# The last down-projection of a two-layer hybrid decoder, computed and stored in halves of 256 tokens

## The reference

```python
for l in range(DEPTH):                     # DEPTH 2, x is (1, 512, 1024), float32
    ...                                    # mixers A to D on head groups
    x = x + mixed @ w_out[l]
    h2 = rmsnorm(x, ln2_g[l])
    g = causal_dwconv(h2 @ ffn_w_gate[l], ffn_conv_w[l])
    x = x + (jax.nn.silu(g) * (h2 @ ffn_w_up[l])) @ ffn_w_down[l]   # 2816 -> 1024
return x
```

## Time and profile before

| what | value |
| --- | --- |
| median of three runs | 1314.4 us |
| span of the profiled execution | 1310.8 us |
| what the median has over that span | 3.6 us |
| TensorE busy, of the span | 98% |
| VectorE, ScalarE, GpSimd busy | 65%, 38%, 49% |
| one addition onto x, 128 x 512 | 685 ns |
| stores of x | 8 of 256 KB, median 4.6 us from issue to landing |

### The profile page before, as it was taken

How to read it: one execution, slowest core, us unless ns; L and a number is a source line. 1 busy time by engine, 2 the same in 40 slices (tenths; PEclk the granted TensorE clock), 3 DMA queues, 4 the chain that set the end, 5 groups by cost and what they waited for, 6 DMA issues and landing times.

```text
span 1310.8 us, 15989 instructions
## 1 busy us (share of the span) xinstructions
PE 1290.9 (98%) x6218; PEld 1054.8 (80%) x6218; DVE 849.4 (65%) x1142; ACT 493.5 (38%) x758; POOL 637.2 (49%) x302
## 2 busy tenths in 40 slices
PE   7999999999999999999999999999999999999999
PEld 4888886787888888888878888867878888888887
DVE  8789885846888117775237799677477761377720
ACT  6332556744223112223344245566432221122220
POOL 2986661144444444444468776512444444444442
PEclk9999999999999999999999999999999999999999
DMA  6232331123333323333232322301333233233332
GB/s 222 81 97 65 97 89 33 28 94 113 97 97 115 101 74 97 97 98 110 84 111 82 87 65 92 87 25 53 99 106 97 97 106 103 81 97 97 109 111 87
DMA packets 40939, 120.49 MB, mean 92 GB/s; under 512 B 6432, under 2 KB 10656, under 8 KB 40864
## 3 DMA queue, kind: packets, MB, share of 16 engines
q1 hardware_dynamic: 40864, 119.46, 29.3%
HBM read 114.20 MB, written 2.10 MB: 89 GB/s over the span
## 4 chain that ended last, share of the span: by engine, by line
PE 90%; DVE 5%; ACT 2%; POOL 2%; DMA 1%; issue 1%; SPq 0%; POOLq 0%; ACTq 0%
PE bank L504 26%; PE bank L517 26%; PE bank L509 25%; PE bank L718 3%; PE bank L506 1%; ACT G L1079 1%; PE bank L766 1%; DMA raw<-in_w_in 1%; POOL wl L362 1%; PE bank L663 1%; PE bank L755 1%; DVE G L1568 1%; PE bank L596 1%; PE bank L611 1%; DVE ssum L1196 1%; PE bank L745 1%
## 5 line engine op out<-in xcount | busy, mean ns | idle before, releaser
L362 POOL TENSOR_TENSOR wl<-raw,wh 128x1024 fp32r<-128x1024 f32 (+3 forms) x208 | 507.1, 2439 | 629.4 <-ACT wh L903 385.1
L903 ACT ACTIVATE wh<-raw 128x1024 fp32r<-128x1024 f32 (+3 forms) x208 | 218.6, 1052 | 267.3 <-PE bank L509 207.9
L504 PE MATMUL bank<-xl,wh 128*128 128x512 f32 x1088 | 282.4, 397 | 0.0
L517 PE MATMUL bank<-xh,wl 128*128 128x512 f32 x1088 | 271.1, 391 | 0.0
L509 PE MATMUL bank<-xh,wh 128*128 128x512 f32 x1056 | 261.0, 389 | 0.0
L504 PEld LDWEIGHTS bank<-xl,wh 128*128 128x128 f32 x1088 | 202.8, 188 | 48.2 <-issue 5.9
L517 PEld LDWEIGHTS bank<-xh,wl 128*128 128x128 f32 x1088 | 203.2, 188 | 41.7
L509 PEld LDWEIGHTS bank<-xh,wh 128*128 128x128 f32 x1056 | 198.3, 188 | 41.5
L1230 DVE TENSOR_TENSOR x<-x,bank 128x512 f32<-128x512 f32 x64 | 43.9, 685 | 228.5 <-PE bank L517 228.4
L504 PE MATMUL bank<-ml,wh 128*128 128x512 f32 x512 | 137.5, 395 | 0.0
L517 PE MATMUL bank<-mh,wl 128*128 128x512 f32 x512 | 127.5, 389 | 0.0
(11 more groups left out here) (304 smaller groups left out, 1357.8 us busy)
## 6 DMA issues: line engine op xcount, KB each, us to landing
raw<-in_w_gu SPq DMA_DIRECT2D x88, 512.0 KB, 3.5
raw<-in_w_in SPq DMA_DIRECT2D x52, 512.0 KB, 3.7
raw<-in_w_dn SPq DMA_DIRECT2D x32, 704.0 KB, 4.1
raw<-in_w_ol SPq DMA_DIRECT2D x16, 384.0 KB, 3.1
raw<-in_w_oe SPq DMA_DIRECT2D x16, 256.0 KB, 2.6
x<-in_x SPq DMA_DIRECT2D x8, 256.0 KB, 6.2
raw<-in_w_first SPq DMA_DIRECT2D x4, 512.0 KB, 3.8
out_x<-x SPq DMA_DIRECT2D x8, 256.0 KB, 4.6
```

Of the source, the lines that this page charges most:

```text
L362: tt(wl[:, p, 0:cols], raw[:, p, 0:cols], wh[:, p, 0:cols].bitcast(F32), ALU.subtract).then_inc(wl_full, 1)
L504: mm(bank[b][:, :], wh[:, p, k * P:(k + 1) * P], lo[:, k, :], start=(k == 0), stop=False)
L517: w = mm(bank[b][:, :], wl[:, p, k * P:(k + 1) * P], hi[:, k, :], start=False, stop=(k == K - 1))
L903: fn(wh[:, p, 0:cols], raw[:, p, 0:cols], ACT.Copy).then_inc(wh_full, 1)
```

## The change

In the last down-projection of the last layer the first unit is left as it is on TensorE; the seven others go through a new function, `halved_unit`. It splits the 512 tokens into two halves of 256 and gives each a bank of its own, b and b + 2. In each of the three groups it does the 11 tiles for the first half and then the 11 for the second, and loads the weights of each tile for each half. After the third group's first half it raises `half_done`, after the second `unit_done`. VectorE adds each half when it is done, and SP stores each half by itself: sixteen stores of 128 KB. The first unit's result is added in two halves as well.

```diff
@@ sync @@
             for i in range(KD):
-                sp.wait_ge(resid, L * 4 * KD - KD + i + 1)
-                sp.dma_start(A["out"][:, i, :], x[:, i, :]).then_inc(out_done, 16)
-            sp.wait_ge(out_done, 16 * KD)
+                for part, signal in ((0, half_resid), (1, resid)):
+                    sp.wait_ge(signal, (L * 4 * KD - KD if part else 0) + i + 1)
+                    cols = slice(part * THALF, part * THALF + THALF)
+                    sp.dma_start(A["out"][:, i, cols], x[:, i, cols]).then_inc(out_done, 16)
+            sp.wait_ge(out_done, 32 * KD)
@@ tensor @@
+            def halved_unit(b, K, hi, lo, out):
+                g = next(number)
+                p = g % 2
+                halves = [(bank[b + 2 * i], slice(i * THALF, i * THALF + THALF)) for i in range(2)]
+                pe.wait_ge(wh_full, g + 1)
+                claim(b, out)
+                claim(b + 2, out, 0)
+                for moving in (lo, hi):
+                    for to, cols in halves:
+                        for k in range(K):
+                            w = mm(to[:, 0:THALF], wh[:, p, k * P:(k + 1) * P], moving[:, k, cols],
+                                   start=(k == 0 and moving is lo), stop=False)
+                w.then_inc(wh_free, 1)
+                pe.wait_ge(wl_full, g + 1)
+                for (to, cols), done in zip(halves, (half_done, unit_done)):
+                    for k in range(K):
+                        w = mm(to[:, 0:THALF], wl[:, p, k * P:(k + 1) * P], hi[:, k, cols], start=False, stop=(k == K - 1))
+                    w.then_inc(done, 1)
...
-                units(8, FHALF, mh, ml, resid, hid_ready)
+                if l + 1 < L:
+                    units(8, FHALF, mh, ml, resid, hid_ready)
+                else:
+                    unit(0, FHALF, mh, ml, resid, hid_ready)
+                    for o in range(1, KD):
+                        halved_unit(o % 2, FHALF, mh, ml, resid)
@@ vector @@
+            def half_residual(o, p):
+                for part, done, signal in ((0, half_done, half_resid), (1, unit_done, resid)):
+                    cols = slice(part * THALF, part * THALF + THALF)
+                    dve.wait_ge(done, nth(done))
+                    tt(x[:, o, cols], x[:, o, cols], bank[p + 2 * part][:, 0:THALF], ADD).then_inc(signal, 1)
...
-                    for o in range(KD):
-                        residual(o, o % 2)
+                    dve.wait_ge(unit_done, nth(unit_done))
+                    for part, signal in ((0, half_resid), (1, resid)):
+                        cols = slice(part * THALF, part * THALF + THALF)
+                        tt(x[:, 0, cols], x[:, 0, cols], bank[0][:, cols], ADD).then_inc(signal, 1)
+                    for o in range(1, KD):
+                        half_residual(o, o % 2)
```

More of the change, by code:

```diff
@@ L16 @@
 D, T, P = 1024, 512, 128
+THALF = T // 2
 KD = D // P
@@ L195, in build @@
         unit_done, unit_out, resid = sem("unit_done"), sem("unit_out"), sem("resid")
+        half_done, half_resid = sem("half_done"), sem("half_resid")
         raw_full = [sem(f"raw_full{p}") for p in range(2)]
```

## The result

The changed kernel takes 1317.17 us (median of 13 runs, 1316.53 to 1317.58) where the kernel before took 1314.4 beside it (13 runs, 1313.72 to 1315.99): a ratio of 1.0019 [1.0011, 1.0027], +2.8 us by the medians, +1.4 to +3.5 by the interval. No change (a ratio of 1) lies outside the interval, so the kernel is slower. Against the prediction's own limit, about 0.2% or 1317.0 us, it stands on the edge: the median is just over it, the ratio just inside. The forecast was 1313.8, faster by 0.6; the rival of a fixed price per pair gave 1316.9.

A forecast was written before the change was run, and what follows sets the result against it. TensorE, busy for 98% of a 1310.8 us span, was taken as the bound. Matmuls 0, tail -0.57 and the rest nothing gave -0.6: span 1310.2, with 3.6 around it 1313.8 us; 8-in-10 range 1312.7 to 1317.6.

The forecast's parts named there:

- a fixed price per pair: Rival: each load-and-matmul pair keeps 13 ns over its columns, so doubled pairs cost +3.1; net +2.5 us, 1316.9; chance 0.32.
- What bounds the kernel: Whole kernel: TensorE, busy 98% of 1310.8 us at full clock, ends last nearly everywhere, up to one final VectorE addition.
- The matmuls: Seven halved outputs, 231 loads more: 256-column pairs at 0.1133 us, 7.48 us an output, so 0; range -0.8 to +3.1.
- the third of the three lines: Sum for one output with 13 ns kept per pair: 66 x 0.1200 = 7.92 us, +0.44, seven times +3.1.
- The lower bound: Spacing of 256-column pairs: at least 0.112 us, what a load of 128 columns occupies in plain float32 rows.
- The tail: After the last matmul: last addition halved -0.27 us, last store halved -0.3; together -0.57 (-0.27 to -0.7).
- The rest at nothing: New waits, sixteen stores, fourteen additions, weight-buffer signals: no cost; at most +0.7 us if TensorE's queue were held at each output.
- The load alone: Rival: the weight load sets the pace in halved outputs, 0.112 us a pair; -1.4 us, 1313.0; chance 0.09.
- slow feed: Rival: TensorE's instructions come too slowly in halved outputs, 0.128 us a pair, 8.43 an output; 1320.5 us; chance 0.07.
- The slow rate of plain float32: Rival: 256-column rounded-float32 matmuls in halved outputs run at 0.215 us a pair; +46 us, 1361; chance 0.04.
- the 3.6 us around the span: Whole run: median 1314.4 us less profiled span 1310.8, taken as unchanged and added to the forecast span.
- the tail's ends: After the last matmul: the range of the gain, -0.27 to -0.7 us, with 0 and -0.4 for the store.

The follow-up runs named there:

- the first experiment: Changed kernel with its seven halved outputs cut at other columns (384+128, 320+192, 272+240, 304+208, 448+64, twice 256+256): 1322.4 us, beside 1314.8 for the kernel before.

## Why the prediction was wrong

**What bounds the kernel**: right. TensorE ends last up to the last addition in both profiles.

**The matmuls: here it failed.** The bound of the sum was right and the choice inside it wrong. The step is "A fixed price for changing weights should be there too, as the same number of weight columns is loaded; it isn't, so I lean to the rest going with the columns". It took 0; measured is +0.44 us an output, +3.08 for seven, the third of the three lines. The argument took the price from one type to another: a plain float32 pair has 2.6 ns over its columns at 256 as well, bfloat16 2.2 to 2.4, and rounded float32 13 at 256 and at 512. The widths between show that the rest doesn't go with the columns. The point that the prediction named as its own end, a pair spaced over 0.1146 us, was passed at 0.1200. What the trace before did hold, the same kind of matmul at 512 columns with 0.0134 over, spoke for itself, and no row gave a reason for that rest to halve.

**The lower bound**: right. The load's 0.112 from plain float32 holds for rounded float32, as the narrow halves of the first experiment show. Here the two types agree, in the price above they don't. It is no bound for bfloat16, whose pairs stand at 0.1091.

**The tail**: right in its size and its parts, -0.57 against 2.56 - 3.15 = -0.59. The last addition reads 0.42 us, the store lands in 1.7 us, and the first half's store, issued at 1312.17 and so 1.32 us ahead of the second at 1313.49, not 0.8, is out of its way. Store and addition give 0.3 each.

**The rest at nothing**: right. There is no idle time ahead of an output's first load in the timeline of after, and TensorE waits for nothing new.

**The rivals.** The fixed price came, as +3.08 - 0.59 = +2.5 us, beside +2.8 [+1.4, +3.5] measured. The load alone would have 7.37 us an output and slow feed 8.4 or more; 7.92 was measured, with no idle put down to issue. 924 instructions in a row at 60 ns each were issued without a gap, and 55 ns each, in the bfloat16 pairs of 0.1091, were reached too. The slow rate of plain float32 doesn't come with short matmuls of rounded float32. Its price in that rival was half of what it is: the prediction counted one pair of 0.215 us for each matmul, and plain float32 has two.

**The frame of the sum**: the 3.6 us around the span were 1.8 us and a start of the profiled run that was about 2 us early. As the sum was a difference, this did not change its sign or size, but the spans of two profiles alone would have put the loss at 4.8 us. Two smaller figures don't come out of their own terms: the tail's ends give the fixed price 1316.8 to 1317.2, not 1316.3 to 1317.6, and 0.124 us a pair gives 1318.7.

## What to carry to other kernels

Before a matmul is split along its moving side, take from the trace the spacing of pairs of the very same type less their columns at the clock, and count that rest once for each added load; a row of another type told nothing of it here. If a split is to bring forward the end of a kernel, split only what lies just ahead of that end: the last six tiles give about the same tail as seven outputs and cost 0.08 us instead of 3.08, by the profiles; that this beats the kernel before is not shown by the times. A gain of half a microsecond at the end is to be read from the tail in the profile, since neither the times nor the spans of single profiles resolve it.

## What the runs showed of the hardware that was not expected

- Rounded float32 with a load for every matmul is spaced about 13 ns over its columns (0.1200 us at 256, 0.2267 at 512; 11 to 18 ns from 272 to 448), where bfloat16 and plain float32 at its half rate have 2 to 3 ns. The cause was not found.
- A plain float32 matmul stands in the trace as two pairs of load and matmul, each at half rate: 0.432 us for 256 columns.
- With 64 or 32 weight columns the same pair is quicker at 256 moving columns (0.1134) and slower at 512 (0.231 and 0.232 against 0.2267).
- The start of a run varies: the first matmul that follows the first weights began between 7.44 and 9.58 us in nine profiles, one for each kernel, and this alone moves a span by some 2 us.
